# ScalarE's copy of head 0's probabilities between the steps of the convolution branch's activation

## The reference

```python
def conformer_branch(pa, conv_w, conv_b, ln_g, ln_b):
    glu = pa[..., :CONV_D] * jax.nn.sigmoid(pa[..., CONV_D:])
    c = causal_dwconv(glu, conv_w, conv_b)
    return jax.nn.silu(layer_norm(c, ln_g, ln_b))

def diff_attention_branch(pq, pk, pv, rel_bias, ...):
    ...                                   # 4 heads, 512 queries in 4 blocks
    logits = einsum(q_blk, k) * scale + bias       # chunk-causal mask
    p = jax.nn.softmax(logits, axis=-1)
    attn = p[:, :, 0] - lam * p[:, :, 1]
    return einsum(attn, v)

def hybrid_mixer(h, ...):
    ...
    merged = (gates[:, :, 0] * (ya @ w_br[0]) + gates[:, :, 1] * (yb @ w_br[1])
              + gates[:, :, 2] * (yc @ w_br[2]))
    return merged @ w_out
```

## Time and profile before

| | us |
|---|---|
| median of three runs (1760.45 to 1761.63) | 1760.96 |
| the profiled execution | 1761.88 |
| its span in the trace | 1760.1 |
| PE busy | 1741.1 (99%) |
| PE weight loads | 1447.8 (82%) |
| DVE busy | 1287.1 (73%) |
| ACT busy | 745.7 (42%) |
| POOL busy | 491.3 (28%) |

### The profile page before, as it was taken

How to read it: one execution, slowest core, us unless ns; L and a number is a source line. 1 busy time by engine, 2 the same in 40 slices (tenths; PEclk the granted TensorE clock), 3 DMA queues, 4 the chain that set the end, 5 groups by cost and what they waited for, 6 DMA issues and landing times. The chain is left out here.

```text
span 1760.1 us, 21739 instructions
## 1 busy us (share of the span) xinstructions
PE 1741.1 (99%) x8127; PEld 1447.8 (82%) x8127; DVE 1287.1 (73%) x1696; ACT 745.7 (42%) x951; POOL 491.3 (28%) x204
## 2 busy tenths in 40 slices
PE   9999899999999999999999998999999999999998
PEld 7888788888888888888888887888888888888888
DVE  7998768664678776577779786775746797685585
ACT  4234555443564443343432345553445544343343
POOL 4453000103034244444133620010030332444440
PEclk9999999999999999999999999999999999999999
DMA  6532244422322332232232323444222223322321
GB/s 216 191 120 72 102 165 137 172 96 96 120 75 94 120 109 85 98 117 82 110 144 72 144 72 120 168 140 148 96 96 96 96 96 120 118 74 96 120 74 71
DMA packets 40777, 199.60 MB, mean 113 GB/s; under 512 B 4828, under 2 KB 14300, under 8 KB 20320
## 3 DMA queue, kind: packets, MB, share of 16 engines
q1 hardware_dynamic: 38460, 186.35, 30.0%
q0 software_dynamic: 1648, 11.54, 1.7%
q10 hardware_dynamic: 564, 0.33, 0.1%
HBM read 186.06 MB, written 14.49 MB: 114 GB/s over the span
## 5 line engine op out<-in xcount | busy, mean ns | idle before, releaser
L1699 PE MATMUL ps<-x_hd,w_hd 128*128 128x512 f32 x1568 | 612.3, 390 | 0.1
L1700 PE MATMUL ps<-x_tl,w_hd 128*128 128x512 f32 x1568 | 610.4, 389 | 0.0
L606 POOL TENSOR_TENSOR w_tl<-raw,w_hd 128x2048 fp32r<-128x2048 f32 x79 | 366.0, 4632 | 534.5 <-ACT w_hd L724 392.6
L724 ACT ACTIVATE w_hd<-raw 128x2048 fp32r<-128x2048 f32 (+2 forms) x159 | 298.1, 1875 | 321.7 <-PE ps L1700 231.9
L1715 PE MATMUL ps<-x_hd,w_tl 128*128 128x512 f32 x1568 | 373.4, 389 | 0.0
L1699 PEld LDWEIGHTS ps<-x_hd,w_hd 128*128 128x128 f32 x1568 | 294.3, 188 | 62.6 <-issue 0.7
L1715 PEld LDWEIGHTS ps<-x_hd,w_tl 128*128 128x128 f32 x1568 | 294.1, 188 | 61.0
L1700 PEld LDWEIGHTS ps<-x_tl,w_hd 128*128 128x128 f32 x1568 | 294.4, 188 | 60.5
L1699 PE MATMUL ps<-ring_hd,w_hd 128*128 128x512 f32 (+1 forms) x640 | 241.1, 381 | 0.0
L1700 PE MATMUL ps<-ring_tl,w_hd 128*128 128x512 f32 (+1 forms) x640 | 239.8, 379 | 0.0
L1402 DVE SCALAR_TENSOR_TENSOR merged<-merged 128x512 f32<-128x512 f32 x44 | 183.4, 4167 | 20.7 <-ACT merged L724 20.2
(11 more groups left out here) (229 smaller groups left out, 1654.0 us busy)
## 6 DMA issues: line engine op xcount, KB each, us to landing
raw<-units SPq DMA_DIRECT2D x154, 1024.0 KB, 4.8
att_dram<-s_sb SPq DMA_DIRECT2D x8, 640.0 KB, 2.9
s_sb<-att_dram SPq DMA_DIRECT2D x32, 160.0 KB, 3.4
bias_t<-bias_tiles POOLq DMA_DIRECT2D x8, 256.0 KB, 5.5
cg<-mem_t POOLq DMA_DIRECT2D x2, 1024.0 KB, 7.2
resid<-x_t POOLq DMA_DIRECT2D x1, 2048.0 KB, 8.1
resid_dram<-resid POOLq DMA_DIRECT2D x1, 2048.0 KB, 7.4
resid<-resid_dram POOLq DMA_DIRECT2D x1, 2048.0 KB, 8.2
```

The source lines that it names most:

```text
L606: line.done(pool.tensor_tensor(w_tl[:, k % 2, :], raw[:, k % 2, :], w_hd[:, k % 2, :].bitcast(F32), ALU.subtract), of_unit("tail", g))
L724: line.done(act.activation(out, in_, func, **kw), *labels)
L1699: pe.matmul(dst, w_hd[:, slot, w], hd[:, src, :], start=kc == 0, stop=False)
L1700: i = pe.matmul(dst, w_hd[:, slot, w], tl[:, src, :], start=False, stop=False)
```

## The change

ACT's copy of head 0's probabilities is taken out of unit 16 and put into the loop of unit 15, behind `th` of tile 1 and ahead of `z` of tile 2. The copies of heads 1 to 3 stay. It happens in both layers. No instruction is added or removed, and no other engine's program changes.

```diff
-IN_ORDER_AT = {ATT0 + 3 * _h + 3: _h for _h in range(HEADS)}
+IN_ORDER_AT = {ATT0 + 3 * _h + 3: _h for _h in range(1, HEADS)}
...
+            def probabilities_in_order(h):
+                act.wait_ge(att_in, 64 * (l * HEADS + h + 1))
+                op(att_t.rearrange("p t (a j) -> p t a j", a=4), moved, labels=(f"att{h}",))
...
                             if k in IN_ORDER_AT:
-                                h = IN_ORDER_AT[k]
-                                act.wait_ge(att_in, 64 * (l * HEADS + h + 1))
-                                op(att_t.rearrange("p t (a j) -> p t a j", a=4), moved, labels=(f"att{h}",))
+                                probabilities_in_order(IN_ORDER_AT[k])
...
                             op(th, z, ACT.Tanh, (f"th_c{i}",), (), scale=0.5)
+                            if i == 1:
+                                probabilities_in_order(0)
```

## The result

The changed kernel takes 1748.40 us (median of six runs, 1748.01 to 1750.23) against 1761.05 for the kernel before (median of six), a ratio of 0.9931 with a 95% interval of 0.9919 to 0.9944. That is 12.65 us faster. The forecast was 1747.0, with a range of 1743.5 to 1753. The profiled execution took 1748.45, its span is 1746.6, so the two profiled executions differ by 13.43 and their spans by 13.5. The lines that are named here are four higher in the changed kernel: L1812 is job D, L1802 the scores, L1719 the pass with the weight's tail, L1323 DVE's read-out of the gates.

A forecast was written before the change was run, and what follows sets the result against it. PE bounds the kernel, standing still before D0 and then running at a slower clock. Gains of 7.38 us in layer 0 and 6.61 in layer 1 sum to 13.99, giving 1747.0 against the median of 1760.96; range 1743.5 to 1753.

The forecast's parts named there:

- The bound and who is late: PE bounds; D0 waits for ACT's copy, losing 5.9 or 5.5 us per layer, plus 2.85 or 2.98 by the slow clock.
- The copy's new place: ACT, unit 15: copy ends at 201.64, D0 starts without wait in layer 0 and waits 0.3 us in layer 1.
- What is pushed back: Gates' read-out behind the copy: new PE wait of 1.4 and 1.6 us before unit 17; 7.38 and 6.61 won.
- the plain reckoning of 17.2: If nothing else stood in the way, unit 17 would start 8.76 and 8.2 to 8.5 us earlier.
- whole gain: Rival: PE doesn't wait for the gates' read-out, or its chain shrinks; 17.2 us go, 1743.8; chance 0.07.
- The clock: PE's remaining gaps, 1.4 and at most 0.3 + 1.6 us per layer, leave the granted clock at 1.00.
- The rival: Clock falls in PE's new bank wait before unit 17, costing 5.8 us and leaving 8.2: 1752.8; chance 0.10.
- What comes late next: DVE reads unit 17's gates out 0.7 us late by PE's reckoning; that lag costs nothing.
- The time: Whole kernel: 1761.88 - 13.99 = 1747.9 for the profiled execution, 1747.0 against the median.
- The rule against it: Skill's advice to wait late for a DMA; its page alone gives 1.8 us more per layer, about 1750.6.
- given back later: Rival: lags behind unit 17 meet less slack and return 3 to 9 us, giving 1750 to 1756; chance 0.08.
- Slower: Rival: copy's wait blocks ACT, each microsecond of later read costs PE one per layer; 10 late gives 1767; chance 0.03.

The follow-up runs named there:

- the filler run: The kernel before, with 24 small matmuls filling PE's standstill ahead of D0, which still waits for the copy: 1756.42 us, beside 1761.2.
- the run with the early read-out: The changed kernel, with DVE's read-out of unit 16's gates moved ahead of the products ya_src of tiles 2 and 3: 1745.45 us, again 1745.57.
- the run with layer 0 alone: The kernel before, with the copy moved in layer 0 only and left in its old place in layer 1: 1754.68 us, beside 1761.36.
- the late reads: The changed kernel, with SP's four reads of head 0 issued behind the load of unit 19 in place of ahead of it: 1756.34 us.
- the run with the early read-out alone: The kernel before, copy in its old place, with only DVE's read-out of unit 16's gates moved ahead of ya_src of tiles 2 and 3: 1757.43 us.

## Why the prediction was right

**The bound and who is late.** Right. The two waits of D0 and the slow clock behind them were what the change could win, and the filler run shows the second apart, with 5.5 us by the traces and 4.8 by the medians for my 5.8.

**The copy's new place.** Right. D0 doesn't wait in layer 0 and waits 0.28 in layer 1, for a forecast of 0.3.

**What is pushed back.** This was the step on which the forecast differed from the plain reckoning of 17.2, and it holds: a new wait of 1.49 us in each layer where I had 1.4 and 1.6. The read-out is what PE waits for, as the run with the early read-out shows, in which unit 17 starts while ACT's Tanh still runs. The early read-out of the gates takes the wait away, and with it comes the "whole gain" of the first rival, 3.0 us further down, by a change that the rival didn't have. The term was a little small: 13.71 measured for 13.99. The layers miss by 0.20 and 0.08, and of the 0.28 about 0.2 is that PE goes on 0.14 after the read-out's end where I had taken 0.04, in both layers.

**The clock.** Right for this kernel: 1.00 behind the gaps of 1.5 us. But the row that I took for it, could not show it, and that part is luck. Its 2 us are the last 0.42 us of PE's work and the first 1.58 us of a standstill, and no matmul follows in which a slower clock could be seen. These are the two stretches that come next, and two out of the long standstill ahead of D0, all of the kernel before (columns as in the earlier trace rows):

```profile
1756.00:1758.00 2.00, 0.00 (x0) 0.63 1.02 337
1758.00:1760.00 2.00, 0.00 (x0) 0.50 0.48 165
...
204.00:206.00 2.00, 0.00 (x0) 1.00 0.00 0
207.00:207.78 0.78, 0.00 (x0) 0.50 0.00 0
```

At the end of the span the mean clock of the next 2 us is 0.63, and in the standstill after which D0 ran at half the clock it still stood at 1.00 from 204 to 206. So a clock of 1.00 within a gap doesn't tell the clock behind it; with the copy behind tile 0 it was 1.00 in the gap of 2.9 us and fell behind it. The rival named a real mechanism. With the copy one tile earlier, the same wait for the same banks was 3 us, the clock fell behind it, and 3.4 us went in both layers together, for the 5.8 that the rival had.

**What comes late next.** Right in kind. DVE reads the gates of unit 17 at 219.75, 1.0 us behind the start of B1 on PE (218.75); before it was 0.11 (225.62 behind 225.51, see the earlier trace rows for the first). It is 0.9 later by PE's reckoning for the 0.7 I had, and PE has no wait there.

**The time.** 1748.4 for 1747.0. The largest part of these 1.4 us is one step of the sum: I had taken off the 0.92 by which the profiled execution lay above its median as well. The changed kernel's profiled execution lies only 0.05 above its own median, so the step misses by 0.87. The table shows why it counts something twice. Outside the two places the traced execution of before (1733.6 us) is no slower than those of the other kernels (1733.5 to 1734.3), so its excess lay, as far as the traces tell, in the two places, in the very 28.31 us from which the 13.99 were taken. The 0.70 us less for D0 and A1 behind the same wait, in the run with layer 0 alone, fit that. Of the rest 0.28 is the chain's, and 0.28 lies outside the two places (13.71 there, 13.43 between the profiled executions).

**The rule against it.** The reads cost nothing extra: the copy starts 3.83 and 4.57 us behind the issue of the last read, for the 3.7 and 4.6 that I had read from the trace of before.

**The other rivals.** Nothing is given back later: layer 0 alone and both layers add up. Slower needs the read to land late, and the late reads show that the price is one to one, as I had it; 7.6 us of lateness in sum left 5.0 of the gain.

## What to carry to other kernels

When a late step on an in-order engine is moved forward, what it jumps over becomes the next bound: count the chain from the step's new end through everything behind it to whoever waits, and compare it with the chain it frees. The best place is where the two end together; here that was one tile later than chosen, and moving a bank's read-out out of the second chain was worth more than any place (3.0 us against 1.3). A difference between one traced execution and the median is not to be taken off a forecast when it may lie in the place that the change removes. A standstill of the matmul engine can cost twice, by its length and by a slower clock behind it (here behind those of 2.9 us and more, not behind those of 1.5), so cutting it can be worth more than the time cut off (3.9 us for 2.8 in the run with the early read-out alone).

## What I had not expected

The granted clock behind a gap of PE, in the traces read here: 1.00 behind gaps of 1.1 and 1.5 us, 1.00 behind gaps of 2.3 and 2.7 in the one traced execution, 0.61 and 0.64 over the next 3 us behind gaps of 2.9 and 3.1, 0.58 and 0.59 over D0 behind gaps of 3.6 to 4.3, and 0.50 behind those of 5.3 to 5.8. D0, which takes 2.3 us at the full clock, took 4.0 to 4.1 and 4.6 in the last two cases. And a filler of matmuls whose result nobody reads was worth 4.8 us.

An event that the trace names as the releaser can be a neighbour. The same wait was put down to ACT's Tanh in one execution and to DVE's read-out in the next, and only a run in which the two lie apart, with unit 17 starting ahead of the Tanh's end, settled it.
